# Head norms of the attention queries: four token blocks on 32 partitions each in place of one row of 512 tokens

## The reference, cut to what matters

```python
def rms_norm(x, g):
    xf = x.astype(jnp.float32)
    y = xf * lax.rsqrt(jnp.mean(xf * xf, axis=-1, keepdims=True) + NORM_EPS)
    return (y * g.astype(jnp.float32)).astype(x.dtype)

# memory_attention:   k = rms_norm(split_heads(k), k_gain);  q = rms_norm(q, q_gain)
# dilated_attention:  q = rms_norm(q, q_gain)
```

## Time and profile before

| what | value |
|---|---|
| median of three runs | 3321.79 us |
| profiled execution, its own time | 3322.76 us |
| its span, first to last instruction | 3320.7 us |
| TensorE busy, share of the span | 3271.2 us, 99% |
| VectorE busy | 1743.1 us, 52% |
| ScalarE busy | 1189.2 us, 36% |
| mean granted TensorE clock | 0.992 |

### The profile page before, as it was taken

One profiled execution on the slowest core, in us unless ns is written; L12 is line 12 of the kernel. 1 busy time (PEld: TensorE's weight loads), 2 busy tenths in 40 slices (PEclk: granted clock), 3 DMA queues, 4 the chain that ended last, 5 costly groups with the idle time before them and its releaser, 6 DMA issues.

```text
span 3320.7 us, 44519 instructions
## 1 busy us (share of the span) xinstructions
PE 3271.2 (99%) x18577; PEld 2617.0 (79%) x18577; DVE 1743.1 (52%) x2551; ACT 1189.2 (36%) x1884; POOL 414.3 (12%) x318
## 2 busy tenths in 40 slices
PE   8999999999999999999999999999999999999999
PEld 6777778887777888887777788888878887678887
DVE  7954456844446443448777544434464335454333
ACT  4344434534542422233233332223353224342221
POOL 0001012001001311113322111101011001011110
PEclk9999999999999999999999899999999999999999
DMA  6732123322122232342100023333323322023332
GB/s 243 232 95 69 53 95 120 114 84 64 58 89 70 90 100 95 96 130 83 52 2 2 27 87 112 97 95 95 96 89 95 95 91 85 7 73 98 99 96 83
DMA packets 83911, 295.47 MB, mean 89 GB/s; under 512 B 9472, under 2 KB 12800, under 8 KB 81664
## 3 DMA queue, kind: packets, MB, share of 16 engines
q1 hardware_dynamic: 78384, 270.61, 25.7%
q10 hardware_dynamic: 5328, 22.02, 2.1%
HBM read 283.94 MB, written 8.65 MB: 88 GB/s over the span
## 4 chain that ended last, share of the span: by engine, by line
PE 90%; DVE 5%; ACT 2%; issue 1%; POOL 0%; DMA 0%; ACTq 0%; DVEq 0%; POOLq 0%
PE acc L485 71%; PE acc L1529 1%; PE aux L1514 1%; PE acc L2515 1%; PE acc L3298 1%; PE aux L1810 1%; PE aux L3260 1%; PE aux L1828 1%; PE acc L1841 1%; PE acc L2519 1%; DVE w_lo L396 1%; PE acc L2502 1%; PE acc L2012 1%; PE aux L2001 1%; PE acc L2468 1%
## 5 line engine op out<-in xcount | busy, mean ns | idle before, releaser
L485 PE MATMUL acc<-op_hi,w_hi 128*128 128x512 f32 x2624 | 1070.0, 408 | 7.2 <-DVE op_lo L1166 3.8
L389 ACT ACTIVATE w_hi<-raw 128x1024 fp32r<-128x1024 f32 (+2 forms) x476 | 494.2, 1038 | 1522.0 <-PE acc L485 1512.1
L485 PE MATMUL acc<-op_hi,w_lo 128*128 128x512 f32 x2624 | 1025.7, 391 | 0.0
L485 PE MATMUL acc<-op_lo,w_hi 128*128 128x512 f32 x2624 | 1024.2, 390 | 0.0
L396 DVE TENSOR_TENSOR w_lo<-raw,w_hi 128x1024 fp32r<-128x1024 f32 (+2 forms) x476 | 574.3, 1206 | 288.5 <-ACT w_hi L389 288.2
L485 PEld LDWEIGHTS acc<-op_hi,w_hi 128*128 128x128 f32 x2624 | 493.9, 188 | 130.9 <-issue 30.1
L485 PEld LDWEIGHTS acc<-op_lo,w_hi 128*128 128x128 f32 x2624 | 494.8, 189 | 106.8 <-issue 10.1
L485 PEld LDWEIGHTS acc<-op_hi,w_lo 128*128 128x128 f32 x2624 | 493.6, 188 | 106.5
L485 PE MATMUL acc<-ffn_hi,w_hi 128*128 128x512 f32 x800 | 311.4, 389 | 0.0
L485 PE MATMUL acc<-ffn_hi,w_lo 128*128 128x512 f32 x800 | 311.2, 389 | 0.0
L485 PE MATMUL acc<-ffn_lo,w_hi 128*128 128x512 f32 x800 | 311.2, 389 | 0.0
(11 more groups left out here) (596 smaller groups left out, 3893.1 us busy)
## 6 DMA issues: line engine op xcount, KB each, us to landing
raw<-in_w SPq DMA_DIRECT2D x436, 512.0 KB, 3.6
late_ada<-in_ada ACTq DMA_DIRECT2D x32, 512.0 KB, 4.4
raw<-in_w SPq DMA_DIRECT2D x32, 384.0 KB, 3.0
ada<-in_ada ACTq DMA_DIRECT2D x4, 1024.0 KB, 14.7
ada<-in_ada SPq DMA_DIRECT2D x4, 1024.0 KB, 21.8
x_mid<-x SPq DMA_DIRECT2D x16, 256.0 KB, 2.9
x<-x_mid SPq DMA_DIRECT2D x2, 2048.0 KB, 7.9
skew<-rel_rows SPq DMA_DIRECT2D x12, 192.0 KB, 3.1
```

Source lines behind the costliest of these rows:

```text
L389: act.activation(self.w_hi[g % AHEAD][:, 0:k, :], self.raw[s][:, 0:k, :], ACT.Copy).then_inc(self.split_hi.handle, 1)
L485: mm = pe.matmul(self.bank(s, g), w[:, k, :], a[:, k, 0:s.n], start=(k == 0 and q == 0), stop=(k == k_tiles - 1 and q == 2))
```

## The change

The 512 tokens are split into four blocks of 128, and block t uses partitions 32t to 32t+31.

- Sums: one product of 128x512 becomes four products of 128x128, each with a window of 32 columns, each writing 32 partitions of the first 128 columns of the bank. The window table grows from 10 to 36 columns; rows of a block that belong to no head become zero.
- Root and reciprocal work on 128 partitions x 128 columns instead of 4 or 6 partitions x 512 columns.
- Spread: two products of 512 columns with 4 or 6 rows become eight products of 128 columns with 128 rows; a column of the identity picks the row 32t+2i+e.
- Planned times: the spreads and the finishing products of `GroupNorms` come 2.4 us earlier, in both uses; the memory attention of the late stage starts 2.4 us earlier in the plan, and with it what is planned from its end. The start of the dilated units is planned as the latest of three times, so it moves from 55.8 to 53.4 us after the planned start of the query projection.
- Two small tables, `sums` and `roots`, shrink from 64 to 16 columns.

```diff
-             "window": np.stack([(i < HD) * (c == 4) + (i >= HD) * (c == 5) for c in range(10)], 1) / HD,
+             "window": np.stack([(i < HD) * (c == 4) + (i >= HD) * (c == 5) for c in range(4 + Q)], 1) / HD,
...
-                act.activation(self.factor[0:2 * n, :], self.sums[0:2 * n, :], ACT.Sqrt, bias=self.eps[0:2 * n, :]
+                act.activation(self.factor[:, 0:P], self.sums[:, 0:P], ACT.Sqrt, bias=self.eps
...
-                pe.matmul(self.sums[0:2 * n, :], core.c("window")[:, 4 - 2 * i:4 - 2 * i + 2 * n], self.square[j % 2],
-                          start=(i == 0), stop=(i == n - 1), skip_group_check=True).then_inc(*self.summed.inc())
+                for t in range(NT):
+                    mm = pe.matmul(self.sums[t * Q:(t + 1) * Q, 0:P], core.c("window")[:, 4 - 2 * i:4 - 2 * i + Q],
+                                   self.square[j % 2][:, t * P:(t + 1) * P], start=(i == 0), stop=(i == n - 1),
+                                   skip_group_check=True)
+                mm.then_inc(*self.summed.inc())
...
-                yield self.at[j - i + n - 1] + 8.4 + 2.0 * i
+                yield self.at[j - i + n - 1] + 6.0 + 2.0 * i
...
-                for e in range(2):
-                    mm = pe.matmul(self.spread[e * HD:(e + 1) * HD, :],
-                                   column(core.c("ident")[0:2 * n, 2 * i + e:2 * i + e + 1], HD),
-                                   self.factor[0:2 * n, :], start=True, stop=True)
+                for t in range(NT):
+                    for e in range(2):
+                        row = t * Q + 2 * i + e
+                        mm = pe.matmul(self.spread[e * HD:(e + 1) * HD, t * P:(t + 1) * P],
+                                       column(core.c("ident")[:, row:row + 1], HD), self.factor[:, 0:P],
+                                       start=True, stop=True)
...
-                    dve.reciprocal(self.factor[0:2 * n, :], self.factor[0:2 * n, :]).then_inc(*self.inverted.inc())
-                yield self.at[j - i + n - 1] + 9.4 + 2.0 * i
+                    dve.reciprocal(self.factor[:, 0:P], self.factor[:, 0:P]).then_inc(*self.inverted.inc())
+                yield self.at[j - i + n - 1] + 7.0 + 2.0 * i
...
-        self.memory.times(taken[1] + 14.0, 3.0)
+        self.memory.times(taken[1] + 11.6, 3.0)
...
-        core.sums = core.sb("sums", [P, 64])
-        core.roots = core.sb("roots", [P, 64])
+        core.sums = core.sb("sums", [P, RET_HEADS * NT])
+        core.roots = core.sb("roots", [P, RET_HEADS * NT])
```

More of the change, by code:

```diff
@@ L64 @@
 ROUND = 1.5 * 2.0 ** 23
+Q = 32
 DECAY_SCALE = -float(np.exp(-0.5))
```

## The result

The changed kernel takes 3301.8 us (median of 7 runs, 3298.89 to 3305.67); 7 runs of the kernel before beside it had a median of 3318.9 us (3310.46 to 3326.87). The ratio is 0.9941, 95% interval 0.9927 to 0.9956: 15 to 24 us saved. Part of the distance is the kernel before itself: its median was 3321.79 us in the three runs that the prediction started from, and 2.9 us less in these seven. Rival 2 (3303.2 us, chance 0.18) comes nearest.

What follows compares the result with a forecast made beforehand. TensorE, busy 99% of the span, was taken to bound the kernel. Sums -4.4, spreads +0.2, projection's end -1.7, earlier attention -0.65, clock -4.0 make -10.55 us from 3321.79: 3311.2, given as 3311.5 us, range 3303 to 3320.

Steps and rivals of the forecast that it cites:

- Rival 2: Layer 0: the clock stays up there too, its 17 us at half clock gone, 8 us more, 3303.2 us; chance 0.18.
- The clock: Late stage: with less idle time the 10.1 us at half clock go, 4.0 us saved, ends 0 and 5.
- the late term: Late stage: the 4.0 us saved by the clock no longer falling to 0.50.
- The sums: All 11 tiles: a sum falls from 0.95 to 0.55 us, 4.4 us saved, ends 0.7 and 6.2.
- rival 3: Sums in all 11 tiles: four blocks run at once, 0.37 us each, 6.4 us saved, 3309.2 us; chance 0.08.
- The lower bound in the prediction: Sums: 0.39 us each, from 64x32 products at 0.029 us and a start of 0.153.
- The spreads: All 11 tiles: 16 products take 1.02 us against 1.00 now, 0.2 us lost.
- Rival 5: All 11 tiles: new products don't overlap in pairs, 3.14 us against 1.95, +10.8 us in all, 3332.6 us; chance 0.08.
- Root, reciprocal, end of the projection, earlier attention: Late stage: shorter reciprocal leaves the chain, 1.7 us net saved; eighth memory unit under the projection, 0.65 us saved.
- The walk's new gap of 1.5 us: After the query projection: walking the queues, TensorE has work until 6.1 us, second exponentials end at 7.6 us; 1.5 us lost.

## Why the prediction was right and wrong

**The clock, the step that failed most.** The prediction gave the late spell to idle time and to "a spread of 6 rows", and counted on less idle time: 4.0 us there, and none for the 17 us in layer 0. The sign of the late term was right by luck, for its reason was wrong: with sums and spreads filled TensorE idles 2.12 us in that stretch, with only the spreads filled 1.43 us, with the long reciprocal put back it waits 1.0 us for that, and the clock stays full all the same. Layer 0's spell, which the prediction let stand, went by the same cause. Rival 2 had named it, with the remark that both spells follow such spreads; its "against" (spreads under the dense projection cause no fall, and the 64x64 products of the RWKV stage run at full clock) was true and yet no objection; why those stretches keep their clock was not measured. What the spreads' rows are worth in runs is 0.25% [0.14, 0.35], 8.3 us; the prediction had 4.0, for the late stage alone.

The Trainium skill ("TensorE: Matmul & The Clock Gate", Part 1) says that the gate follows how busy TensorE has recently been. Here a busy TensorE wasn't enough: at 2858 to 2868 us it had no idle time and 0.50 of the clock, and zeros in more rows raised the clock with no instruction added on TensorE.

**The sums.** Taken at 0.55 us by the 64-column row, measured at 0.36: rival 3's 0.37. Two tiles in one run take 0.57, so eight more instructions cost 0.21, 0.026 each, half of the 0.054 of the 64-column shape and a quarter of a full-width product's 0.11; the rest, 0.15, is the start that the prediction had. The saving on TensorE is 11 x (0.95 - 0.36) = 6.5 us in place of 4.4. The lower bound in the prediction, 0.39 from the 64x32 products at 0.029, came near by luck: their 32 are moving columns, not weight columns.

The Trainium skill ("TensorE: Matmul & The Clock Gate", Part 3) says that products on different column groups run at the same time. The 0.026 us agrees with that for four groups; no run puts the same four blocks on one column group to compare.

**The spreads.** 1.02 us for 16, as forecast (0.90 to 1.09 in layer 0). Rival 5 is out.

**Root, reciprocal, end of the projection, earlier attention.** The durations are as forecast, 0.37 and 0.94 us, and the reciprocal left the chain. The savings were mis-sized. The prediction took whole pieces of the chain for time that would go, 3.18 and 0.65 us, while TensorE had other work beside most of them: all its idle time there was 1.88 us, the waits of 1.2 and 0.7 us shown with the plan. The walk's new gap of 1.5 us did not come either, since TensorE is busy from 2834 to 2847 us. The 1.41 us idle at the projection's end are near the 1.5 by luck: 1.18 of them lie ahead of the root, where TensorE waits for the scaled memory output, and 0.23 behind it. And the earlier plan, put down as 0.65 us saved, brought that wait and the one of 1.43 us under the projection. In place of 1.7 + 0.65 us saved, the late stage idles 1.1 us longer than before.

**The sum.** The profiled pair can be taken apart by the two stretches of dense products that hold the norms: layer 0's before and after, then the late stage's before, after, and after with the old plan.

```profile
1532.10:1924.40 392.30, 380.10 (x4994) 302.87 (x4993) 269.82 (x583) 140.50 (x262) 93.53 (x110) 0.97 0.08 26
1531.20:1912.90 381.70, 369.59 (x5048) 299.00 (x5047) 265.63 (x582) 139.99 (x262) 84.64 (x110) 0.99 0.08 27
```
```profile
2762.20:2939.60 177.40, 171.17 (x925) 122.52 (x924) 89.54 (x215) 63.80 (x177) 5.30 (x4) 0.96 0.10 29
2750.70:2919.80 169.10, 161.74 (x1068) 125.61 (x1067) 83.39 (x215) 62.61 (x177) 5.17 (x4) 0.99 0.10 31
2748.00:2917.60 169.60, 165.24 (x1069) 128.38 (x1067) 81.99 (x215) 62.73 (x177) 5.85 (x4) 0.97 0.10 30
```

In layer 0's stretch 27.3 us were at 0.50 before and 10.2 after, in the late one 13.7 and 3.4. If half of such time is lost, an estimate, the 10.6 us of layer 0 are 8.5 of clock, 2.0 of work and 0.1 of waiting, and the 8.2 us of the late stage are 5.1 of clock and 4.2 of work, less 1.1 of added waiting. The work, 6.2 us, is what the sums saved less what the spreads cost. So the clock gave some 13.7 us where the prediction had 4.0, the sums 6.5 where it had 4.4, the spreads took 0.2 as forecast, and the waits took about 1 where it had 2.35 saved. The runs agree on the clock: its mean is 0.9958 in the six runs of the changed kernel unaltered and 0.9923 in the 17 beside them, by the same estimate 11.8 of the 18.3 us between their means. That is more than the 8.3 us of the filled spreads alone, but with six runs it is uncertain by some 3 us, and the tables' 0.18% [0.07, 0.30] may hold a part of it. The two comparisons of the changed kernel, 0.59% [0.44, 0.73] and 0.51% [0.37, 0.65], are 17 to 20 us. Rival 2's 3303.2 us came so near with the right cause, but also because its errors cancel: its sums are too small and its waits too favourable.

## What to carry to other kernels

When the granted clock falls while TensorE is busy, look at how many of the 128 rows the products just before it feed; zero rows cost no time here (1.01 us for a spread against 1.00) and kept the clock up, and a kernel with only such zeros added is a cheap test. A small product of few output columns can be split over column groups: here four blocks of 32 columns took 0.36 us in place of 0.95. A piece of another engine in the chain is worth no more than TensorE's idle time beside it: 3.83 us of pieces stood against 1.88 us of idle time. And look at what an earlier plan puts on the path before crediting it: here it brought 2.6 us of waits for the 0.7 that it took away.

## What the hardware showed beyond what was expected

- In the two places behind the norms the clock fell behind spreads with 6 rows in 10 windows of 10, and with 128 rows in none of 18, by the table above. Under the dense projection spreads of 4 and 6 rows cause no fall (clock 1.00 from 2772 to 2844 us, with the spread at 2792.98). How few rows are too few, and beside what work, was not measured.
- The number of weight columns of a sum of 512 moving columns hardly counts. All 11 sums take 10.4 us of the chain with 4 or 6 columns (the kernel before) and 10.4 us with 128 (only the sums filled); single ones lie at 0.95 and at 0.86 to 1.09 us. The 1 us that one expectation above drew from 0.86 against 0.95 is not there.
- Other sizes of three tables, with no instruction of TensorE changed, gave 0.18% [0.07, 0.30]; the cause is open.
